# Modulation sums of the four late groups: 16 split fp32r products in one strip of rows become 8 plain fp32 products in four column groups

## The chip, the cores and the metric

The kernel runs on one core of one Trainium2 chip. The metric is device microseconds (us) of one execution. Before the change the median of 3 runs is 2868.03 us (2867.95 to 2868.06).

## The reference, cut to what matters

The program is one layer of a hybrid trunk: adaLN modulation, an input projection, a recurrent branch and a differential attention branch, an output projection, and an expert-choice mixture of 16 experts. The change touches only how the modulation vectors are made:

```
def modulation(cvec, w_mod, b_mod):
    m = jax.nn.silu(cvec) @ w_mod + b_mod
    return m[..., None, :]
...
sh1, sc1, g1, sh2, sc2, g2 = jnp.split(mod, 6, axis=-1)
h = rmsnorm(x, lp['g_pre1']) * (1 + sc1) + sh1
t, k, v, h_fin = token_mixer(h, ...)
x = x + g1 * rmsnorm(t, lp['g_post1'])
h = rmsnorm(x, lp['g_pre2']) * (1 + sc2) + sh2
f = expert_choice_ffn(h, ...)
x = x + g2 * rmsnorm(f, lp['g_post2'])
```

There are two conditioning vectors (latent and context, v = 0 and 1), D = 2048, and w_mod is 2048 x 12288. The first two of the six parts (sh1, sc1) are needed at once. The other four, "late groups" g = 0 to 3 (g1, sh2, sc2, g2), are needed only after the token mixer.

## The kernel before, in words

All work is in one program for five engines: TensorE (PE) multiplies, VectorE (DVE) and ScalarE (ACT) do elementwise work, and two queues start the transfers, SyncE (SP) for the large weights and GpSimd (POOL) for results and small loads. Every engine runs its own list in order and waits on semaphores.

A stage of 32 units makes the first 4096 columns of the input projection. A unit u is 128 columns of w_in. PE's loop in `block.tensor` runs over four groups g of eight units n, and for each unit over two halves of 320 tokens with 48 matmuls each (`unit_piece`, lines 2362 to 2364). Since fp32 weights are split in a high and a low fp32r part, ACT makes `w_hi` (`split_hi`, line 405) and DVE makes `w_lo` (`split_lo`, line 415) of a unit while PE works on the unit before; each is one instruction over 128x2048. `w_hi` and `w_lo` have two buffers, so the split of unit u + 1 starts when PE has left unit u - 1.

Beside this, group g also makes late modulation group g. The 16 row tiles of w_mod (128x2048, 1 MB each) go through three buffers `mod_raw`; SP issues their loads in `mod_tiles` (line 605). DVE multiplies each tile by the two columns of silu(c) and accumulates in `mod_acc` (`mod_tile`, lines 1559 and 1561, two instructions a tile). `MOD_TILES` says how many of the 16 tiles are taken in each of the eight units of a group: 3, 3, 3, 3, 2, 2, 0, 0. What is left is a sum over the 128 partitions, for two rows of 2048. For it ACT copies `mod_acc` to `acc_hi` at n = 6 (line 1071), DVE subtracts to `acc_lo` at n = 7 (`mod_low`, line 1576), and after unit 7 PE runs `sum_mod`: for four blocks of 512 columns and two v, a product with `acc_hi` and one with `acc_lo`, stationary `sel` 128x2, output on partitions 0 and 1 of PSUM banks 0 to 3 (lines 2375 and 2376). In unit 1 of the next group DVE adds the bias (`mod_row2`, line 1584), and POOL, which waits for it, stores the rows to `d_mod` (line 823).

`acc_hi` and `acc_lo` lie where `mod_raw` lies, so SP waits for the semaphore `mod_summed` before it loads the first three tiles of the next group (line 604).

After the 32nd unit PE runs the fourth sum and goes on with head 0 of the attention stage. After its third piece of 12 matmuls that head turns the keys (`keys`), which need `k_past` and `k`, loaded by POOL in its step u = 31 (lines 793 and 790).

Of the kernel before, what the change touches and what calls it, by code (L numbers as in the profile page):

```python
# [61 lines left out]
NMOD = 3  # L62
MOD_TILES = (3, 3, 3, 3, 2, 2, 0, 0)
MOD_FROM = [sum(MOD_TILES[:n]) for n in range(8)]

# [47 lines left out]
def trunk(nc, a, out_ctx, out_lat, out_k, out_v, out_state):  # L113
    ctx = ExitStack()
    with ctx:
# [42 lines left out]
        def place(at0, items):  # L158

            o, made = at0, {}  # L160
            for name, shape, dt in items:
# [14 lines left out]
                       ("sp_a", [P, 16], F32), ("sp_b", [P, 16], F32), ("sp_c", [P, 16], F32),  # L176
                       ("sp_d", [P, 16], F32), ("A1", [P, 2, KT], F32), ("ones2", [P, 4], F32)])
        mod_at = PLACED["ones2"] + 64
        A["sc"] = at("sc", [P, 32], F32, mod_at + NMOD * UB)
        sel = at("sel", [P, 2, 2], F32R, mod_at + NMOD * UB + 128)  # L180
        mod_raw = at("mod_raw", [P, NMOD, D], F32, mod_at)
# [3 lines left out]
        mod_acc = at("mod_acc", [P, 2, D], F32, s0 + 15360)  # L185
        acc_hi = at("acc_hi", [P, 2, D], F32R, mod_at)
        acc_lo = [at("acc_lo0", [P, D], F32R, mod_at + 2 * UB), at("acc_lo1", [P, D], F32R, s0)]
        m_row2 = at("m_row2", [2, D], F32, s0)
        m_row3 = at("m_row3", [2, D], F32, raw_at + 2 * UB)
        assert s0 + 15360 + 2 * UB <= PLACED["rows1"] and mod_at + NMOD * UB + 192 <= s_end  # L190
# [135 lines left out]
            "sqrt_x", "xn_ready", "x_turned", "xt_act", "xt_dve", "b_loaded", "m_row_ready", "m_stored",  # L326
            "zero_stored", "row_act", "start_used", "cols_taken", "mod_used", "mod_hi", "mod_lo", "mod_summed", "rows3_turned", "a1_ready", "tok_hi", "tok_lo",

# [227 lines left out]
        def _(sp):  # L556
# [39 lines left out]
            def mod_tiles(g, n):  # L596

                for k in range(MOD_FROM[n], MOD_FROM[n] + MOD_TILES[n]):
                    if k >= NMOD:
                        wait(sp, "mod_used", g * KT + k + 1 - NMOD)  # L600
                    else:
                        wait(sp, "mod_used", g * KT)
                        if g:
                            sp.wait_ge(S["mod_summed"], g)
                    sp.dma_start(mod_raw[:, k % NMOD, :], w_mod[k * P:(k + 1) * P, (g + 2) * D:(g + 3) * D]
                                 ).then_inc(mod_loaded[k % NMOD], 16)
# [129 lines left out]
        def _(pool):  # L736
# [59 lines left out]
            def load_values(h):  # L796
# [3 lines left out]
                               ).then_inc(S["v_loaded"], 16)  # L800

            for u in range(32):
                wait(pool, "in_taken", 2 * (u + 1))
                pool.dma_start(d_proj[u * P:(u + 1) * P, :], stage[:, u % 2, :]).then_inc(S["in_stored"], 16)
                if u == 31:
                    pool.wait_ge(S["mod_lo"], 8)
                    load_past(0)
                    load_rows(0, "k", 24, "k_loaded")
                stored("in_stored", (u + 1) * 16, "stage_free")
                if u == 26:  # L810
                    pool.wait_ge(S["zero_stored"], TT * 16)
                    load_recurrent(0)
                if u == 30:
                    pool.wait_ge(lo_ready, 2 * NRAW + 2 * (Q_IN * NRAW + 30 + 1))
                    pool.dma_start(m_row3[:], a["b_mod"][0:1, 5 * D:6 * D].to_broadcast([2, D])
                                   ).then_inc(S["b_loaded"], 16)
                if u % 8 == 7 and u < 31:
                    g = u // 8
                    pool.wait_ge(S["mod_summed"], g + 1)
                    pool.dma_start(m_row2[:], a["b_mod"][0:1, (g + 2) * D:(g + 3) * D].to_broadcast([2, D])  # L820
                                   ).then_inc(S["b_loaded"], 16)
                    wait(pool, "m_row_ready", g + 3)
                    pool.dma_start(d_mod[:, (g + 2) * D:(g + 3) * D], m_row2[:]).then_inc(S["m_stored"], 16)
            pool.sem_inc(phase, 1)
# [3 lines left out]
            wait(pool, "m_row_ready", 6)  # L828
            pool.dma_start(d_mod[:, 5 * D:6 * D], m_row3[:]).then_inc(S["m_stored"], 16)
            pool.wait_ge(S["m_stored"], 4 * 16)  # L830

# [140 lines left out]
        def _(act):  # L972
# [87 lines left out]
            for u in range(32):  # L1060
# [352 lines left out]
        def _(dve):  # L1413
# [7 lines left out]
            dve.memset(A["ones_row"][:], 1.0).then_inc(S["const_set"], 1)  # L1421
            own.done(dve.memset(A["ones2"][:], 0.0))
            own.settle()
            own.done(dve.memset(A["ones2"][:, 0:4:3], 1.0))
            own.settle()
            dve.tensor_copy(sel[:], A["ones2"][:].rearrange("p (v m) -> p v m", v=2)).then_inc(S["const_set"], 1)
            dve.wait_ge(S["rows_turned"], 1)
# [121 lines left out]
            def mod_tile(g, k):  # L1549
# [17 lines left out]

            def mod_low(g):

                dve.wait_ge(S["mod_hi"], g + 1)  # L1570
                if g == 0:
                    dve.wait_ge(S["v_stored"], 4 * 16)
                else:
                    dve.wait_ge(S["m_stored"], g * 16)
                for v in range(2):
                    TTn(acc_lo[v][:], mod_acc[:, v, :], acc_hi[:, v, :].bitcast(F32), ALU.subtract
                        ).then_inc(S["mod_lo"], 1)

            def mod_row2(g):

                dve.wait_ge(S["mod_summed"], g + 1)
                dve.wait_ge(S["b_loaded"], (g + 1) * 16)
                m = (m_row3 if g == 3 else m_row2)[:].rearrange("p (b n) -> p b n", b=4)
                TTn(m, ps[0:2, 0:4, :], m, ALU.add).then_inc(S["m_row_ready"], 1)

# [35 lines left out]
            for u in range(32):  # L1621
# [10 lines left out]
                if n == 7:  # L1632
                    mod_low(g)
                if u == 31:
# [20 lines left out]
            def head(h, final):  # L1655
# [89 lines left out]
                def take_T(qt):  # L1745

                    wait(dve, "pdT_hi", h * TT + qt + 1)
                    if qt == 0:
                        dve.wait_ge(S["m_stored"], 4 * 16)
                    if qt < TT - 1:  # L1750
# [464 lines left out]
        def _(pe):  # L2215
# [565 lines left out]
```

## Time and profile before

| what | value |
|---|---|
| median of 3 runs | 2868.03 us |
| span of the profiled execution | 2865.5 us |
| what lies around the span, as median less span | 2.5 us |
| PE busy | 2801.7 us, 98% of the span |
| DVE, ACT, POOL busy | 74%, 53%, 10% |
| stage of 32 units and four sums on PE | 194.0 to 663.5 us |
| granted TensorE clock, mean of the span | 0.991 of full speed |

The profile is of one execution, and its page gives the span from the first to the last instruction; the device time of that execution is taken as the span and the same 2.5 us around it. A matmul's row is its start and its modelled duration. Matmuls overlap, so what one costs is the distance from its start to that of the next, not its duration. Idle time in brackets stands before the row, with what ended it.

### The profile page before, as it was taken

How to read it: one execution, taken by the hardware profiler on the slowest of the kernel's cores; microseconds unless marked ns; L12 is line 12 of the kernel's file. 1: busy time of each engine (PE TensorE's matmuls, PEld its weight loads, DVE VectorE, ACT ScalarE, POOL GpSimd, SP SyncE). 2: the span in 40 equal slices, each digit the busy share in tenths (PEclk: the TensorE clock that was granted, in tenths of full speed). 3: DMA queues.
4: the chain of work that ended last, by engine and by line, in shares of the span. 5: the costliest groups of instructions: out<-in, count | busy, mean ns of one | idle time of the engine just before them, and what ended most of it. 6: DMA issues, size and time to landing. Idle time of an engine off the chain costs nothing.

```text
span 2865.5 us, 42985 instructions
## 1 busy us (share of the span) xinstructions
PE 2801.7 (98%) x15938; PEld 2465.4 (86%) x15938; DVE 2130.4 (74%) x1927; ACT 1512.7 (53%) x1484; POOL 285.5 (10%) x346
## 2 busy tenths in 40 slices
PE   7999999999999999999999996999999999999998
PEld 5689999999999999999998774888888888888886
DVE  2349779796777777763344577888888888888898
ACT  4411221215556655552233445777777777777776
POOL 1000000002111111100000001010111001110100
PEclk9999999999999999999999997999999999999999
DMA  9878669674343333364343766999999999999997
GB/s 367 312 268 258 225 190 303 206 236 143 123 122 115 116 118 114 110 208 135 119 137 121 267 233 247 362 396 395 396 396 397 390 395 395 394 390 386 391 393 298
DMA packets 301484, 757.07 MB, mean 264 GB/s; under 512 B 20376, under 2 KB 184768, under 8 KB 237072
## 3 DMA queue, kind: packets, MB, share of 16 engines
q1 hardware_dynamic: 277280, 650.01, 62.0%
q0 software_dynamic: 23200, 100.72, 10.9%
q10 hardware_dynamic: 928, 5.33, 0.5%
q8 instruction: 48, 0.79, 0.1%
q14 instruction: 28, 0.23, 0.0%
HBM read 700.61 MB, written 55.37 MB: 264 GB/s over the span
## 4 chain that ended last, share of the span: by engine, by line
PE 84%; DVE 8%; DMA 4%; issue 3%; ACT 1%; DVEq 0%; SPq 0%; ACTq 0%; POOLq 0%
PE ps L536 16%; PE ps L538 16%; PE ps L537 16%; PE ps L2362 8%; PE ps L2363 7%; PE ps L2364 7%; DVE mod_acc L1561 4%; PE ps L2493 3%; PE ps L2494 3%; PE ps L2495 3%; DMA mod_raw<-in_w_mod 2%; PE ps L2219 2%; DMA raw<-in_w_mod 1%; PE ps L2431 1%; DVE rsd L1787 1%
## 5 line engine op out<-in xcount | busy, mean ns | idle before, releaser
L461 DVE TENSOR_TENSOR we_lo<-raw,we_hi 128x2048 fp32r<-128x2048 f32 x384 | 877.2, 2289 | 114.3 <-ACT we_hi L456 113.9
L456 ACT ACTIVATE we_hi<-raw 128x2048 fp32r<-128x2048 f32 x384 | 736.5, 1919 | 261.0 <-PE ps L538 261.0
L2362 PE MATMUL ps<-hi,w_lo 128*128 128x320 f32 x2048 | 642.2, 314 | 3.4 <-DVE w_lo L415 3.4
L2363 PE MATMUL ps<-lo,w_hi 128*128 128x320 f32 x2048 | 632.7, 309 | 0.0
L2364 PE MATMUL ps<-hi,w_hi 128*128 128x320 f32 x2048 | 632.6, 309 | 0.0
L415 DVE TENSOR_TENSOR w_lo<-raw,w_hi 128x2048 fp32r<-128x2048 f32 x115 | 263.4, 2291 | 185.7 <-ACT w_hi L405 180.2
L536 PE MATMUL ps<-we_hi,xs_lo 128*128 128x512 f32 x1024 | 399.4, 390 | 0.1
L538 PE MATMUL ps<-we_hi,xs_hi 128*128 128x512 f32 x1024 | 399.2, 390 | 0.0
L537 PE MATMUL ps<-we_lo,xs_hi 128*128 128x512 f32 x1024 | 399.1, 390 | 0.0
L2362 PEld LDWEIGHTS ps<-hi,w_lo 128*128 128x128 f32 x2048 | 384.5, 188 | 12.6 <-issue 6.7
L2363 PEld LDWEIGHTS ps<-lo,w_hi 128*128 128x128 f32 x2048 | 384.7, 188 | 0.2
L2364 PEld LDWEIGHTS ps<-hi,w_hi 128*128 128x128 f32 x2048 | 384.5, 188 | 0.0
L405 ACT ACTIVATE w_hi<-raw 128x2048 fp32r<-128x2048 f32 x115 | 219.8, 1911 | 221.7 <-PE ps L538 135.3
L1561 DVE SCALAR_TENSOR_TENSOR mod_acc<-mod_raw,sc,mod_acc 128x2048 f32<-128x2048 f32 x120 | 276.7, 2347 | 4.9 <-DMA mod_raw<-in_w_mod 1.0
L536 PEld LDWEIGHTS ps<-we_hi,xs_lo 128*128 128x128 f32 x1024 | 192.7, 188 | 41.8 <-issue 0.7
L538 PEld LDWEIGHTS ps<-we_hi,xs_hi 128*128 128x128 f32 x1024 | 192.7, 188 | 40.2
L537 PEld LDWEIGHTS ps<-we_lo,xs_hi 128*128 128x128 f32 x1024 | 192.7, 188 | 39.5
L536 PE MATMUL ps<-we_hi,hid_lo 128*128 128x512 f32 x512 | 201.3, 393 | 0.4 <-DVE hid_lo L2126 0.4
L538 PE MATMUL ps<-we_hi,hid_hi 128*128 128x512 f32 x512 | 199.5, 390 | 0.0
L537 PE MATMUL ps<-we_lo,hid_hi 128*128 128x512 f32 x512 | 199.3, 389 | 0.0
L2493 PE MATMUL ps<-hi,w_lo 128*128 128x320 f32 x512 | 158.5, 310 | 0.3 <-DVE mix L1829 0.2
L2495 PE MATMUL ps<-hi,w_hi 128*128 128x320 f32 x512 | 158.2, 309 | 0.0
(439 smaller groups left out, 3877.4 us busy)
## 6 DMA issues: line engine op xcount, KB each, us to landing
raw<-in_w_e_gate SPq DMA_DIRECT2D x128, 1024.0 KB, 8.0
raw<-in_w_e_up SPq DMA_DIRECT2D x128, 1024.0 KB, 7.6
raw<-in_w_e_down SPq DMA_DIRECT2D x128, 1024.0 KB, 12.0
raw<-in_w_in SPq DMA_DIRECT2D x144, 512.0 KB, 5.4
mod_raw<-in_w_mod SPq DMA_DIRECT2D x64, 1024.0 KB, 5.4
raw<-in_w_mod SPq DMA_DIRECT2D x64, 512.0 KB, 7.5
raw<-in_w_o SPq DMA_DIRECT2D x64, 512.0 KB, 4.9
d_proj<-stage POOLq DMA_DIRECT2D x32, 320.0 KB, 3.4
```

Source lines behind the costliest of these rows:

```text
L415: dve.tensor_tensor(w_lo[:, j % NHL, s], raw[:, slot, s], w_hi[:, j % NHL, s].bitcast(F32), ALU.subtract).then_inc(lo_ready, 1 if fine else 2)
L456: act.activation(we_hi[:, k % NEH, :], raw_slot(k), ACT.Copy).then_inc(hi_ready, 2)
L461: TTn(we_lo[:, k % NEH, :], raw_slot(k), we_hi[:, k % NEH, :].bitcast(F32), ALU.subtract).then_inc(lo_ready, 2)
L536: pe.matmul(out, s_lo, m_hi, start=start, stop=False)
L537: pe.matmul(out, s_hi, m_lo, start=False, stop=False)
L538: return pe.matmul(out, s_hi, m_hi, start=False, stop=stop)
L1561: last = STT(mod_acc[:, v, :], w, c, mod_acc[:, v, :], ALU.mult, ALU.add)
L2362: pe.matmul(out, wl, hi[:, k, ms], start=(k % 16 == 0), stop=False)
L2363: pe.matmul(out, wh, lo[:, k, ms], start=False, stop=False)
L2364: last = pe.matmul(out, wh, hi[:, k, ms], start=False, stop=(k == KT - 1))
L2493: pe.matmul(out, wl, hi[:, k, ms], start=(kk == 0), stop=False)
L2495: last = pe.matmul(out, wh, hi[:, k, ms], start=False, stop=(kk == 7))
```

## The change

The low part, the high part and `sel` go. PE waits for `mod_used`, the count of tiles accumulated, and multiplies `mod_acc` itself, as plain fp32. The stationary operand is 32 columns wide (`pick_row`: a window of a row of zeros with a one at column 1, so that v lands on row v of each strip), the output block j of 512 columns goes to partitions 32j to 32j + 31 of PSUM bank 0. The bias and the rows of the result have the same layout, so the bias is loaded and the result stored by two transfers each, onto a tile that POOL clears first. `mod_raw` is no longer shared; only DVE's first product of a group waits for `mod_summed`. The tiles are spread as 2, 2, 3, 2, 2, 3, 2, 0. POOL's first loads for head 0 wait for the fourth sum, and no longer for the low part of it.

```
-MOD_TILES = (3, 3, 3, 3, 2, 2, 0, 0)
+MOD_TILES = (2, 2, 3, 2, 2, 3, 2, 0)
...
-        acc_hi = at("acc_hi", [P, 2, D], F32R, mod_at)
-        acc_lo = [at("acc_lo0", [P, D], F32R, mod_at + 2 * UB), at("acc_lo1", [P, D], F32R, s0)]
-        m_row2 = at("m_row2", [2, D], F32, s0)
-        m_row3 = at("m_row3", [2, D], F32, raw_at + 2 * UB)
+        m_row2 = at("m_row2", [P, 512], F32, s0)
+        m_row3 = at("m_row3", [P, 512], F32, raw_at + 2 * UB)
...  (SP, mod_tiles)
                         wait(sp, "mod_used", g * KT)
-                        if g:
-                            sp.wait_ge(S["mod_summed"], g)
...  (SP, u == 31)
                     sp.wait_ge(S["mod_summed"], 4)
+                    sp.wait_ge(S["m_stored"], 3 * 32)
...  (POOL)
+            def load_bias(g, row):
+                pool.memset(row[:], 0.0).then_inc(pool_own, 1)
+                pool.wait_ge(pool_own, g + 2)
+                for v in range(2):
+                    pool.dma_start(row[v:P:32, :], quarters(a["b_mod"][0, (g + 2) * D:(g + 3) * D])
+                                   ).then_inc(S["b_loaded"], 16)
+            def store_modulation(g, row):
+                for v in range(2):
+                    pool.dma_start(quarters(d_mod[v, (g + 2) * D:(g + 3) * D]), row[v:P:32, :]
+                                   ).then_inc(S["m_stored"], 16)
...
                 if u == 31:
-                    pool.wait_ge(S["mod_lo"], 8)
+                    pool.wait_ge(S["mod_summed"], 4)
                     load_past(0)
...  (ACT)
-                if u % 8 == 6:
-                    wait(act, "mod_used", (u // 8 + 1) * KT)
-                    act.activation(acc_hi[:], mod_acc[:], ACT.Copy).then_inc(S["mod_hi"], 1)
...  (DVE, mod_tile)
                 if k:
                     own.settle()
+                elif g:
+                    dve.wait_ge(S["mod_summed"], g)
...
-            def mod_low(g):
-                dve.wait_ge(S["mod_hi"], g + 1)
-                ...
-                for v in range(2):
-                    TTn(acc_lo[v][:], mod_acc[:, v, :], acc_hi[:, v, :].bitcast(F32), ALU.subtract
-                        ).then_inc(S["mod_lo"], 1)
...  (DVE, mod_row2)
-                TTn(m, ps[0:2, 0:4, :], m, ALU.add).then_inc(S["m_row_ready"], 1)
+                TTn(m, ps[:, 0, :], m, ALU.add).then_inc(S["m_row_ready"], 1)
...  (PE, sum_mod)
-                pe.wait_ge(S["mod_lo"], (g + 1) * 2)
+                wait(pe, "mod_used", (g + 1) * KT)
...
-                for b in range(4):
-                    s = slice(b * 512, (b + 1) * 512)
-                    for v in range(2):
-                        pe.matmul(ps[0:2, b, :], sel[:, v, :], acc_hi[:, v, s], start=(v == 0), stop=False)
-                        last = pe.matmul(ps[0:2, b, :], sel[:, v, :], acc_lo[v][:, s], start=False, stop=(v == 1))
+                for v in range(2):
+                    for j in range(4):
+                        last = pe.matmul(ps[32 * j:32 * j + 32, 0, :], A["pick_row"][:, 1 - v:33 - v],
+                                         mod_acc[:, v, j * 512:(j + 1) * 512], start=(v == 0), stop=(v == 1))
```

On DVE, the end of group 0 and the start of group 1 (before; the two `w_lo` in one row are units 7 and 8, the third is unit 9):

```order
L415 TENSOR_TENSOR w_lo<-raw,w_hi 128x2048 x2
L1576 TENSOR_TENSOR acc_lo_92<-mod_acc,acc_hi 128x2048
L1576 TENSOR_TENSOR acc_lo_93<-mod_acc,acc_hi 128x2048
L415 TENSOR_TENSOR w_lo<-raw,w_hi 128x2048
L1559 TENSOR_SCALAR mod_acc<-mod_raw,sc 128x2048 x2
L1561 SCALAR_TENSOR_TENSOR mod_acc<-mod_raw,sc,mod_acc 128x2048 x4
L415 TENSOR_TENSOR w_lo<-raw,w_hi 128x2048
L1584 TENSOR_TENSOR m_row_94<-ps,m_row_94 2x2048
L1561 SCALAR_TENSOR_TENSOR mod_acc<-mod_raw,sc,mod_acc 128x2048 x6
```

The same place on DVE after the change (the first row is the last two tiles of group 0, at n = 6):

```order
L1569 SCALAR_TENSOR_TENSOR mod_acc<-mod_raw,sc,mod_acc 128x2048 x4
L412 TENSOR_TENSOR w_lo<-raw,w_hi 128x2048 x2
L1567 TENSOR_SCALAR mod_acc<-mod_raw,sc 128x2048 x2
L1569 SCALAR_TENSOR_TENSOR mod_acc<-mod_raw,sc,mod_acc 128x2048 x2
L412 TENSOR_TENSOR w_lo<-raw,w_hi 128x2048
L1581 TENSOR_TENSOR m_row_90<-ps,m_row_90 128x512
L1569 SCALAR_TENSOR_TENSOR mod_acc<-mod_raw,sc,mod_acc 128x2048 x4
L412 TENSOR_TENSOR w_lo<-raw,w_hi 128x2048
L1569 SCALAR_TENSOR_TENSOR mod_acc<-mod_raw,sc,mod_acc 128x2048 x6
```

Between `w_lo` of one unit and of the next there are now 4, 4, 6, 4, 4, 6, 4 and 0 products instead of 6, 6, 6, 6, 4, 4, 0 and 0, and the two subtractions are gone.

On POOL, the last units of the stage and the first loads of head 0 (before; `m_row_95` is `m_row3`):

```order
L804 DMA d_proj<-stage 128x640 x4
L815 DMA m_row_95<-in_b_mod 2x2048
L804 DMA d_proj<-stage 128x640
L793 DMA k_past<-in_cache_k 128x128
L790 DMA k<-d_proj 128x640
L790 DMA q_in<-d_proj 128x640
```

The same place on POOL after the change:

```order
L816 DMA d_proj<-stage 128x640 x4
L803 MEMSET m_row_91 128x512
L806 DMA m_row_91<-in_b_mod 4x512 x2
L816 DMA d_proj<-stage 128x640
L789 DMA k_past<-in_cache_k 128x128
L786 DMA k<-d_proj 128x640
L786 DMA q_in<-d_proj 128x640
```

The order of the loads is the same; what the load of `k_past` waits for is another semaphore.

## Rows read from the trace of the kernel before

**Rows 1.** The page: busy time (share of the span) and instructions of PE.
```profile
PE 2801.7 (98%) x15938; PEld 2465.4 (86%) x15938; DVE 2130.4 (74%) x1927; ACT 1512.7 (53%) x1484; POOL 285.5 (10%) x346
```

**Rows 2.** PE's waits, 190 to 680 us: us in total, times, longest.
```profile
PE ps L2362 <- DVE w_lo L415: 3.4, 3, 1.4
```

**Rows 3.** Timeline of PE, first sum: start us, us, engine, line, operation.
```profile
306.51 0.31 PE L2364 MATMUL ps<-hi,w_hi 128*128 128x320 f32 x1
306.66 0.39 PE L2375 MATMUL ps<-acc_hi,sel 128*2 128x512 f32 x1
...
310.13 0.39 PE L2376 MATMUL ps<-acc_lo,sel 128*2 128x512 f32 x1
...
310.36 0.30 PE L2362 MATMUL ps<-hi,w_lo 128*128 128x320 f32 x1
```

**Rows 4.** Timeline of PE, start stage: two modulation units between value products.
```profile
97.95 0.40 PE L538 MATMUL ps<-w_hi,hi 128*128 128x512 f32 x1
98.28 1.92 PE L2242 MATMUL ps<-raw,c 128*32 128x512 f32 x16
100.13 0.50 PE L536 MATMUL ps<-w_hi,lo 128*128 128x512 f32 x1
100.47 0.39 PE L537 MATMUL ps<-w_lo,hi 128*128 128x512 f32 x1
```

**Rows 5.** Timeline of PE, tail: plain fp32 products over the full width.
```profile
2851.81 1.88 PE L2750 MATMUL ps<-t_out,ident 128*128 128x512 f32 x4
2853.53 1.88 PE L2753 MATMUL ps<-gained,spread 128*128 128x512 f32 x4
```

**Rows 6.** Timeline of DVE, group 1.
```profile
309.20 2.29 DVE L415 TENSOR_TENSOR w_lo<-raw,w_hi 128x2048 fp32r<-128x2048 f32 x1 [3.88 <-ACT w_hi L405]
315.72 2.48 DVE L1559 TENSOR_SCALAR mod_acc<-mod_raw,sc 128x2048 f32<-128x2048 f32 x2 [4.22 <-DMA mod_raw<-in_w_mod]
...
365.17 14.02 DVE L1561 SCALAR_TENSOR_TENSOR mod_acc<-mod_raw,sc,mod_acc 128x2048 f32<-128x2048 f32 x6
379.39 2.29 DVE L415 TENSOR_TENSOR w_lo<-raw,w_hi 128x2048 fp32r<-128x2048 f32 x1 [0.20 <-DVE mod_acc L1561]
381.60 9.31 DVE L1561 SCALAR_TENSOR_TENSOR mod_acc<-mod_raw,sc,mod_acc 128x2048 f32<-128x2048 f32 x4
```

**Rows 7.** Timeline of the SP queue, start of group 1.
```profile
310.61 1.29 SPq L605 DMA_DIRECT2D mod_raw<-in_w_mod  x3
```

**Rows 8.** Stretch of group 0's eight units: us, busy of PE, PEld, DVE, ACT, POOL.
```profile
194.00:306.50 112.50, 112.50 (x768) 112.47 (x767) 94.82 (x44) 24.63 (x24) 5.20 (x9) 1.00 0.70 222
```

**Rows 9.** Timeline of PE, start of unit 5 of group 1.
```profile
380.60 0.31 PE L2364 MATMUL ps<-hi,w_hi 128*128 128x320 f32 x1
381.82 0.41 PE L2362 MATMUL ps<-hi,w_lo 128*128 128x320 f32 x1 [0.92 <-DVE w_lo L415]
382.07 0.30 PE L2363 MATMUL ps<-lo,w_hi 128*128 128x320 f32 x1
```

**Rows 10.** Timeline of POOL and PE, end of the stage and head 0.
```profile
661.32 0.55 POOL L793 DMA_DIRECT2D k_past<-in_cache_k  x1
661.86 0.54 POOL L790 DMA_DIRECT2D k<-d_proj  x1
663.31 0.40 PE L2376 MATMUL ps<-acc_lo,sel 128*2 128x512 f32 x1
668.84 0.27 PE L2219 MATMUL ps<-ident,k_past 128*128 128x128 f32 x1
```

**Rows 11.** Tile k, 655 to 680 us; then issues by line, whole run.
```profile
DMA to landing us min/median/max: 3.3/3.3/3.3
...
k<-d_proj POOLq DMA_DIRECT2D x8, 320.0 KB, 5.0
```

**Rows 12.** Line 2242, all of its loads: duration ns min/median/max.
```profile
L2242 PEld LDWEIGHTS ps<-raw,c x256: 106/109/178, 10.5 to 118.1; 128*32 128x32 f32 x128
```

**Rows 13.** The page: GB/s moved in 40 slices.
```profile
GB/s 367 312 268 258 225 190 303 206 236 143 123 122 115 116 118 114 110 208 135 119 137 121 267 233 247 362 396 395 396 396 397 390 395 395 394 390 386 391 393 298
```

More of the change, by code:

```diff
@@ L176, in trunk @@
                        ("sp_a", [P, 16], F32), ("sp_b", [P, 16], F32), ("sp_c", [P, 16], F32),
-                       ("sp_d", [P, 16], F32), ("A1", [P, 2, KT], F32), ("ones2", [P, 4], F32)])
-        mod_at = PLACED["ones2"] + 64
+                       ("sp_d", [P, 16], F32), ("A1", [P, 2, KT], F32), ("pick_row", [P, 48], F32)])
+        mod_at = PLACED["pick_row"] + 192
         A["sc"] = at("sc", [P, 32], F32, mod_at + NMOD * UB)
-        sel = at("sel", [P, 2, 2], F32R, mod_at + NMOD * UB + 128)
         mod_raw = at("mod_raw", [P, NMOD, D], F32, mod_at)
@@ L326, in trunk @@
             "sqrt_x", "xn_ready", "x_turned", "xt_act", "xt_dve", "b_loaded", "m_row_ready", "m_stored",
-            "zero_stored", "row_act", "start_used", "cols_taken", "mod_used", "mod_hi", "mod_lo", "mod_summed", "rows3_turned", "a1_ready", "tok_hi", "tok_lo",
+            "zero_stored", "row_act", "start_used", "cols_taken", "mod_used", "mod_summed", "rows3_turned", "a1_ready", "tok_hi", "tok_lo",
             "bank_done", "bank_taken", "v_stored", "in_a_done", "in_taken", "in_stored",
@@ L800, in load_values, with quarters @@
                                ).then_inc(S["v_loaded"], 16)
+            def quarters(x):
+                return x.rearrange("(j n) -> j n", j=4)
+            def load_bias(g, row):
[8 more added lines that the diff above has]
+                                   ).then_inc(S["m_stored"], 16)
             for u in range(32):
@@ L814, in _ @@
                     pool.wait_ge(lo_ready, 2 * NRAW + 2 * (Q_IN * NRAW + 30 + 1))
-                    pool.dma_start(m_row3[:], a["b_mod"][0:1, 5 * D:6 * D].to_broadcast([2, D])
-                                   ).then_inc(S["b_loaded"], 16)
+                    load_bias(3, m_row3)
                 if u % 8 == 7 and u < 31:
                     g = u // 8
-                    pool.wait_ge(S["mod_summed"], g + 1)
-                    pool.dma_start(m_row2[:], a["b_mod"][0:1, (g + 2) * D:(g + 3) * D].to_broadcast([2, D])
-                                   ).then_inc(S["b_loaded"], 16)
+                    if g:
+                        pool.wait_ge(S["m_stored"], g * 32)
+                    load_bias(g, m_row2)
                     wait(pool, "m_row_ready", g + 3)
-                    pool.dma_start(d_mod[:, (g + 2) * D:(g + 3) * D], m_row2[:]).then_inc(S["m_stored"], 16)
+                    store_modulation(g, m_row2)
             pool.sem_inc(phase, 1)
@@ L828, in _ @@
             wait(pool, "m_row_ready", 6)
-            pool.dma_start(d_mod[:, 5 * D:6 * D], m_row3[:]).then_inc(S["m_stored"], 16)
-            pool.wait_ge(S["m_stored"], 4 * 16)
+            store_modulation(3, m_row3)
+            pool.wait_ge(S["m_stored"], 4 * 32)
             def load_head(h):
@@ L1421, in _ @@
             dve.memset(A["ones_row"][:], 1.0).then_inc(S["const_set"], 1)
-            own.done(dve.memset(A["ones2"][:], 0.0))
+            own.done(dve.memset(A["pick_row"][:], 0.0))
             own.settle()
-            own.done(dve.memset(A["ones2"][:, 0:4:3], 1.0))
-            own.settle()
-            dve.tensor_copy(sel[:], A["ones2"][:].rearrange("p (v m) -> p v m", v=2)).then_inc(S["const_set"], 1)
+            dve.memset(A["pick_row"][:, 1:2], 1.0).then_inc(S["const_set"], 1)
             dve.wait_ge(S["rows_turned"], 1)
@@ L1566, in mod_tile @@
                 wait(dve, "mod_used", g * KT + k + 1)
-            def mod_low(g):
-                dve.wait_ge(S["mod_hi"], g + 1)
[L1571 to L1574, printed above, removed]
-                for v in range(2):
-                    TTn(acc_lo[v][:], mod_acc[:, v, :], acc_hi[:, v, :].bitcast(F32), ALU.subtract
-                        ).then_inc(S["mod_lo"], 1)
             def mod_row2(g):
                 dve.wait_ge(S["mod_summed"], g + 1)
-                dve.wait_ge(S["b_loaded"], (g + 1) * 16)
-                m = (m_row3 if g == 3 else m_row2)[:].rearrange("p (b n) -> p b n", b=4)
-                TTn(m, ps[0:2, 0:4, :], m, ALU.add).then_inc(S["m_row_ready"], 1)
+                dve.wait_ge(S["b_loaded"], (g + 1) * 32)
+                m = (m_row3 if g == 3 else m_row2)[:]
+                TTn(m, ps[:, 0, :], m, ALU.add).then_inc(S["m_row_ready"], 1)
             prm, att = C["prm"], C["att"]
@@ L1631, in _ @@
                         conv(0, step)
-                if n == 7:
-                    mod_low(g)
                 if u == 31:
@@ L1748, in take_T @@
                     if qt == 0:
-                        dve.wait_ge(S["m_stored"], 4 * 16)
+                        dve.wait_ge(S["m_stored"], 4 * 32)
                     if qt < TT - 1:
```

## The prediction

> **What bounds the kernel now.** I read the busy times first: PE is busy for 2801.7 of 2865.5 us [rows 1], so a microsecond moves the end only if PE spends or waits it, and DVE, ACT and POOL count only where PE waits for them. Then I read PE's waits in the stage that the change touches. They are three waits for `w_lo`, 3.4 us in all [rows 2]. Last I read the timeline at one sum, at one of the waits, and at the entry to head 0. The reader should see there that PE goes from the last matmul of unit 7 into the sum with no gap and from the sum straight into the next unit [rows 3]: the sum lies on the path with all its length, and what prepares it (ACT's copy, DVE's two subtractions) doesn't.
>
> **The sum on PE.** Before: from the first product at 306.66 to the first matmul of the next unit at 310.36, 3.70 us for 16 products of 512 columns [rows 3]. There are four such sums, and the other three have the same form.
>
> After: 8 plain fp32 products, stationary 128x32, moving 128x512, onto four strips of 32 partitions of one bank, two rounds that accumulate. The trace has just that form in the start stage: line 2242. Two modulation units in a row are 8 such products, recorded as 16 since each fp32 product leaves two records. They stand between fp32r products: last one before at 97.95, the 16 records from 98.28, first one after at 100.13, the next at 100.47 [rows 4]. A product of 512 columns takes 0.231 us from start to start (3.70 / 16). So the eight take from 97.95 + 0.23 = 98.18 to 100.47 - 0.23 = 100.24, that is 2.06 us, with what it costs to enter and leave. That the four strips run side by side follows from the full-width fp32 product: 1.72 us for two of them, 0.86 each [rows 5], so eight in a row would be 6.9 us, and eight in four strips 1.7 us, which with 0.33 us of entry and exit is the 2.06.
>
> The gain is 3.70 - 2.06 = 1.64 us a sum, 6.6 us for four. Its bounds: 3.70 - 1.72 = 1.98 us a sum if entry and exit cost nothing (7.9), and 1.2 us a sum if the change between forms costs twice what the row shows (4.8). I take 6.6.
>
> [...]
>
> **The three waits.** Before, DVE falls behind in units 0 to 4 of groups 1 to 3. Its first tile waits 4.22 us for a transfer [rows 6] that SP could issue only at 310.61, behind `mod_summed` [rows 7]. Then each unit of three tiles takes DVE 14.02 + 0.20 + 2.21 = 16.43 us (365.17 to 381.60) [rows 6]. Eight PE units are 768 matmuls in 112.5 us, 14.06 a unit [rows 8]. DVE has `w_lo` of unit 5 ready at 381.6, and PE begins that unit 1.22 us after its last matmul instead of 0.15, and its second comes 0.25 instead of 0.15 us later [rows 9]: 1.07 + 0.10 = 1.17 us. The page counts 0.92 there, since a modelled end runs past the next start; so the three that it puts at 3.4 us are worth about 3.4 + 3 x 0.25 = 4.2 us.
>
> After, I follow DVE from the start T of PE's unit 0 in group 1. PE leaves unit 7 at T - 2.1. ACT's and DVE's splits of unit 9 follow that by 4.7 us before (306.7 to 311.4) [rows 3, 6], so DVE is free at T + 2.6. The tiles are there, since their buffers are free from the end of group 0. Two tiles with the first product (2.48 for two of line 1559, 4.67 for two of line 1561): T + 10. Each later `w_lo` is ready at its unit's start + 4.6 at best. A unit of two tiles costs DVE 2.2 + 9.5 = 11.7 us, of three 16.4. At n = 2 DVE starts `w_lo` at T + 30.5 and is done with three tiles at T + 47; it makes `w_lo` for unit 4 at T + 49.2, due at T + 56.2. At n = 5 the same: done at T + 89, `w_lo` for unit 7 at T + 91.5, due at T + 98.4. The least margin is 7 us, so all three waits go, 4.2 us. With the last tile at T + 101 and the sum at T + 112.4, the new wait for `mod_used` is over 11 us early. Bounds: 0 (waits stay) and 4.2.
>
> **What lies beside other work.** ACT loses a copy of 128x4096 and DVE two subtractions of 128x2048 a group; DVE's bias add goes from 2048 to 512 elements a partition. PE waited for none of them [rows 2], so they count 0; the smaller add only widens DVE's margin. POOL gets a memset and two small transfers more a group; it works behind PE and its loads in the stage have two buffers of `stage` for cover. If that cover were gone, the cost would be the 1 to 1.5 us that they issue for, each group, on ACT's copies, not on PE at first.
>
> **The moved wait at head 0.** Before, POOL issues `k_past` at 661.32 and `k` at 661.86, behind the store of unit 31, and the keys are turned at 668.84 [rows 10]. After, both stand behind the fourth sum. With the end E of unit 31 at 659.84 (663.31 + 0.23 - 3.70), the sum ends at E + 2.1, POOL sees it some 0.4 us later, issues `k_past` at E + 2.5 and `k` at E + 3.0, where before it was E + 2.0. `k` lands 3.3 us after issue as it did here, or 5.0 as in the median of eight [rows 11]: E + 6.3 to E + 8.0. The keys are due at E + 2.1 + 5.3 = E + 7.4. So the price is 0 to 0.6 us; behind it only the third piece of head 0 and what follows on PE would queue. I take 0, the near value being that of this very load. `q_in`, `gr` and `v` wait for the store of unit 31 as before, and SP's `rope` for `mod_summed`, as before.
>
> **Sum.** 6.6 + 4.2 - 0 = 10.8 us. Against the profiled execution, span 2865.5 and 2.5 around it, 2868.0 - 10.8 = 2857.2 us; the median of the runs, 2868.03, is the same to 0.1, so I predict 2857.2.
>
> **Rivals.**
> *The waits stay.* If the three-tile units or SP's order still make DVE late once a group, only the sums pay: 2868.0 - 6.6 = 2861.4. For it: a three-tile unit is still longer than a PE unit, by 2.4 us. Against it: each is followed by units 2.4 us shorter than PE's, and the late start by 4.22 us is gone. 0.10.
> *Head 0 starves.* The loads land late by 0.6 to 1.5 us; 2858 to 2859. For it: margin of only 1.1 us at the fast landing. 0.09.
> *The strips take turns.* If the four strips shared the array one after another for these operands (they have the same stationary window and all stream one tile, unlike line 2242), a sum would take 8 x 0.86 + 0.3 = 7.2 us in place of 3.70, 14 us more in four, less 4.2 of waits: 2877.8, slower. It decides once a sum is over 3.70 + 4.2 / 4 = 4.75 us. Against it stands the row of the same form. 0.04.
> *The loads of the strips don't hide.* If each of the 16 loads of 0.107 us [rows 12] stood alone, a sum would be 1.72 + 0.3 + 1.7 = 3.7 us, no gain on it, and the total 4.2: 2863.8. The rows speak against it: 16 records with their loads fit in 1.85 us, 0.13 over the bare streaming. [...] 0.03.
> *Given back later.* The experts' stage moves 390 to 397 GB/s [rows 13] and might set the end by itself. Against it: those loads follow PE's use of the buffers, so they come earlier with it. If it held for half the gain: 2862.6 to 2868. 0.05.
>
> **How the numbers follow.** The forecast as worked out has 0.69, with its own range 2855.5 to 2859.0 (bounds 7.9 and 4.8 for the sums, entry 0 to 0.6). I widen to 2854.5 at the low side, for a microsecond of what I can't see, and to 2862.5 at the high side, which takes in the waits that stay and head 0. Below the 0.2% line, 5.7 us, which is about what a measurement of this kernel tells from no change, lies everything under 2862.3: 0.69 + 0.10 + 0.09 and a little of the last, 0.89. Same 0.06, from the loads and the giving back. Slower 0.05.
>
> **What would show it.** In the profile after: eight products (16 records) of form 128*32, 128x512 per sum, about 2.1 us from the last matmul of unit 7 to the first of the next unit; no PE wait for `w_lo` in the stage; DVE's first tile of a group waiting for no transfer; stage end at 663.5 - 10.8 = 652.7 us; ACT without the copy of 128x4096; PE's turn of `k_past` 5.3 us after head 0 begins. The prediction is wrong if a sum takes over 2.6 us, if a wait for `w_lo` or for `mod_raw` on DVE still reaches PE, if head 0 opens with a wait, or if the stage ends 10 us earlier and the end of the program doesn't.

## The result

| kernel | median (us) | lowest to highest | executions |
|---|---|---|---|
| before | 2868.42 | 2866.02 to 2875.65 | 20 |
| after | 2873.99 | 2871.65 to 2875.72 | 20 |

After over before is 1.0017, with a 95% interval of 1.001 to 1.0023: slower by about 5 us, where 2857.2 was predicted. The time lies outside the range. The direction, slower, had a chance of 0.05; by the line of 0.2% (5.7 us) that the prediction draws, this is "same", which had 0.06.

### The profile page after: what moved, and what is told of

It is laid out like the page before. It is cut to its first block, busy times and chain, and to the rows that moved or that the text cites. A ratio compares the mean times of both kernels' runs of the same rounds, so it can differ in the third digit from the quotient of the medians.

```text
span 2873.9 us, 42975 instructions
## 1 busy us (share of the span) xinstructions
PE 2801.5 (97%) x15938; PEld 2466.8 (86%) x15938; DVE 2107.7 (73%) x1918; ACT 1498.9 (52%) x1480; POOL 293.3 (10%) x358
## 3 DMA queue, kind: packets, MB, share of 16 engines
q0 software_dynamic: 23456, 100.72, 10.8%
## 4 chain that ended last, share of the span: by engine, by line
PE 91%; DVE 4%; DMA 2%; ACT 2%; issue 2%; SPq 0%; DVEq 0%; ACTq 0%; POOL 0%; POOLq 0%
PE ps L533 16%; PE ps L535 16%; PE ps L534 16%; PE ps L2357 10%; PE ps L2359 10%; PE ps L2358 10%; PE ps L2487 3%; PE ps L2489 3%; PE ps L2488 3%; PE ps L2214 2%; PE ps L2425 1%; DMA raw<-in_w_mod 1%; DVE rsd L1782 1%; PE ps L2237 1%; PE ps L2226 1%
```

## The profile after

The page, to be set beside [rows 1], and one DMA queue. The queue's columns are packets, MB and share of the 16 engines; its packets of 16 KB are the fetches of instructions, of which the kernel before made 48.

```profile
span 2873.9 us, 42975 instructions
PE 2801.5 (97%) x15938; PEld 2466.8 (86%) x15938; DVE 2107.7 (73%) x1918; ACT 1498.9 (52%) x1480; POOL 293.3 (10%) x358
q8 instruction: 75, 1.23, 0.2%
```

PE's waits from 190 to 690 us, where [rows 2] had three of 3.4 us in all:

```profile
PE ps L2357 <- DVE w_lo L412: 10.9, 3, 3.7
PE ps L2214 <- DMA k<-d_proj: 1.3, 1, 1.3
```

The view still shows three waits for `w_lo`, three times as long. The timelines of PE and DVE at the first sum, to be set beside [rows 3] and [rows 6], show that they aren't the old ones: they stand behind the sums, not in the middle of a group.

```profile
307.98 0.31 PE L2359 MATMUL ps<-hi,w_hi 128*128 128x320 f32 x1
308.22 1.92 PE L2369 MATMUL ps<-mod_acc,pick_row 128*32 128x512 f32 x16
313.82 0.63 PE L2357 MATMUL ps<-hi,w_lo 128*128 128x320 f32 x1 [3.68 <-DVE w_lo L412]
314.25 0.47 PE L2358 MATMUL ps<-lo,w_hi 128*128 128x320 f32 x1
314.51 0.47 PE L2359 MATMUL ps<-hi,w_hi 128*128 128x320 f32 x1
...
319.40 0.31 PE L2357 MATMUL ps<-hi,w_lo 128*128 128x320 f32 x1
```

```profile
310.66 2.29 DVE L412 TENSOR_TENSOR w_lo<-raw,w_hi 128x2048 fp32r<-128x2048 f32 x1 [11.75 <-ACT w_hi L402]
312.87 2.82 DVE L1567 TENSOR_SCALAR mod_acc<-mod_raw,sc 128x2048 f32<-128x2048 f32 x2
```

The releaser that the profile names is a wrong one. The `w_lo` of 310.66 is that of unit 9; the one that PE's matmul at 313.82 reads, of unit 8, DVE began at 296.6 and had by 298.9. PE had its data for 15 us and stood still 3.68 us. What it waited for is in the rows of PE's sequencer (PEldq), which hold PE's semaphore waits, register operations and branches. Line 2374 is the `Fori` of the loop over the groups, and its `COMPARE_BRANCH` is the branch at the end of a turn. Here are the whole run and then the first turn alone (duration ns min/median/max, starts in us):

```profile
L2374 PEldq COMPARE_BRANCH  x4: 83/4996/5030, 308.3 to 669.0; - x4
```

```profile
L2374 PEldq COMPARE_BRANCH  x1: 5030/5030/5030, 308.3 to 308.3; - x1
```

The same line of the kernel before:

```profile
L2380 PEldq COMPARE_BRANCH  x4: 83/210/240, 306.5 to 659.7; - x4
```

The branch back to the loop's start took 5.0 us in each of three turns, where it took 0.21 to 0.24; the fourth, not taken, costs 0.08 in both. The first one ended at 313.36, and the next matmul began 0.46 us later. Between 305 and 330 us the instruction queue moved four blocks of 16 KB after the change, and between 300 and 330 none before:

```profile
q8 instruction: 4, 0.07, 1.6%
```

Windows around the first stall (us, busy of PE, PEld, DVE, ACT, POOL, granted clock, DMA share, GB/s), and the second window of the second turn:

```profile
308.00:313.80 5.80, 2.14 (x18) 0.44 (x17) 3.14 (x2) 2.23 (x2) 0.61 (x2) 0.87 0.40 146
313.80:319.20 5.40, 5.38 (x20) 5.38 (x21) 5.31 (x4) 0.00 (x0) 2.25 (x3) 0.50 0.49 147
319.20:325.00 5.80, 5.80 (x42) 5.80 (x41) 1.20 (x1) 0.44 (x1) 0.00 (x0) 1.00 1.11 353
```

```profile
434.60:440.00 5.40, 5.40 (x26) 5.40 (x27) 5.31 (x4) 0.00 (x0) 2.28 (x3) 0.68 0.47 144
```

After the 3.7 us in which PE was idle the granted clock is 0.50 of full speed: matmuls of 320 columns follow each other by 0.267 us instead of 0.147 for 20 of them, 2.4 us more. That is why PE's busy time hardly fell although its work did.

The fourth sum leaves the loop and doesn't branch back. Behind it stands what was forecast for all four; then comes the turn of the keys, with a wait (beside [rows 10]); and the load of `k` took 5.7 us (beside [rows 11]):

```profile
668.85 1.92 PE L2369 MATMUL ps<-mod_acc,pick_row 128*32 128x512 f32 x16
670.70 0.41 PE L2357 MATMUL ps<-hi,w_lo 128*128 128x320 f32 x1
...
677.50 0.33 PE L2214 MATMUL ps<-ident,k_past 128*128 128x128 f32 x1 [1.26 <-DMA k<-d_proj]
```

```profile
671.10 0.56 POOL L789 DMA_DIRECT2D k_past<-in_cache_k  x1 [0.84 <-PE ps L2369]
671.65 0.54 POOL L786 DMA_DIRECT2D k<-d_proj  x1
```

```profile
DMA to landing us min/median/max: 5.7/5.7/5.7
```

The account of the two profiled executions, by the start of the sums: before 306.66, 424.16, 542.15, 659.84, distances of 117.50, 117.99, 117.69; after 308.22, 429.05, 548.96, 668.85, distances of 120.83, 119.91, 119.89. The three turns lost 3.33 + 1.92 + 2.20 = 7.45 us. The stage began 1.46 us later, which lies ahead of all that is changed; the fourth sum gained 1.6 and head 0 lost 1.4. Together that is 8.7 us, where the spans differ by 8.4.

## The experiments

Three theories stood at first. A, placement: the branch costs a fetch because of where the loop lies among the blocks in which PE's instructions are fetched. B, the sum itself: its products in column groups hold the sequencer, and what comes behind them is late wherever it lies. C, the reading that the profile itself gives: DVE is late with `w_lo`. A became D in the course of this. A fetch is one packet of 16 KB, a block. In the placed kernel that comes next the last six of the first turn begin from 198.62 to 290.57 us, 18.4 us apart in the mean, and a turn has 1598 records of PE and takes 114.69 us; so a block holds 256 instructions (18.39 x 1598 / 114.69), an estimate that takes one record for one instruction. D supposes that PE keeps eight such blocks, and that the loop, of 1598 instructions, ends just inside its eighth; some time after the sequencer enters that block the ninth is fetched over the first. By D a branch back that comes sooner finds the first block (below, a hit), and a later one has to fetch it (a miss).

**after_slot176.** The loop's first instruction is put at place 176 of a block, so that the loop lies in seven blocks (176 + 1598 = 1774 of 1792). Nothing else changes.

```
-            with pe.Fori(0, 4) as g:
+            with nc.Fori(0, 4, engines=[mybir.EngineType.PE], head_slot={mybir.EngineType.PE: 176}) as g:
```

> The changed kernel, with PE's loop of the 32 units loaded so that its first instruction stands at slot 176 of a block of 256 instructions (1598 instructions, so it ends at slot 1774 of 1792 in its seventh block). Nothing else differs. Theory A (place of the loop in the fetched blocks): the backward branch, 5.03 us three times in the changed kernel against 0.24 before, hits again, the instruction queue q8 moves 48 packets and not 75, no half clock in the stage; time 2874.0 less 3 x 3.7 us of waiting and some 6 us of half clock, that is 2857 to 2860. Theory B (the column-group products in front of the branch hold PE's sequencer, wherever the loop lies): the branch stays at 5 us, 2873 to 2875. Theory C (DVE is late with w_lo, as the page's releaser says): nothing changes, 2874.

Measured: 2858.41 us (2857.29 to 2859.47), ratio to before 0.9964 (0.9949 to 0.9978; the brackets behind a ratio are its 95% interval). The branches, the queue, and the timeline at the first sum:

```profile
L2374 PEldq COMPARE_BRANCH  x5: 83/215/339, 190.1 to 650.9; - x5
```

```profile
q8 instruction: 49, 0.80, 0.1%
```

```profile
306.52 0.31 PE L2359 MATMUL ps<-hi,w_hi 128*128 128x320 f32 x1
306.76 1.92 PE L2369 MATMUL ps<-mod_acc,pick_row 128*32 128x512 f32 x16
308.62 0.42 PE L2357 MATMUL ps<-hi,w_lo 128*128 128x320 f32 x1
```

The fifth branch is the one into the placed loop. The sums stand 114.69, 114.68 and 114.69 us apart: 768 matmuls in 112.5 and 2.2 for the sum, with no wait in between. Against the unplaced kernel a turn lost 3.74 us of idle and 2.4 of half clock in the first, 3.7 and 1.5 in the other two, 16.5 us in all; the medians differ by 15.6. B, the sum as the cause wherever the loop lies, falls, and C with it.

**before_slot176.** The same placement in the kernel before: is it worth something by itself?

> The kernel before, with the start of PE's late loop placed so that neither the loop's last instructions nor its branch come near the end of the eighth block of 256 instructions. It is the control of the placement alone. Theory D (a missed loop back edge is what costs, and the kernel before hits all three of its own by default): three branches of 0.21 to 0.24 us as before, 48 or 49 instruction fetches, and the kernel before's time, 2868 us within 0.2%; the runs of the kernel before that lie up to 7 us above its median (2875.65 us was the slowest) should be missing here if they were executions in which back edges missed. Rival (the placement itself is worth the 10 us that the changed kernel gained by it): 2858 us.

Measured: 2867.39 (2866.34 to 2869.32), ratio 0.9994 (0.9985 to 1.0003). No change: the placement by itself is worth nothing that these runs show, and it pays where the branch missed.

**before_slot216 and before_slot239.** The kernel before with its branch 22 and 45 instructions into the eighth block.

```
+            with nc.Fori(0, 4, engines=[mybir.EngineType.PE], head_slot={mybir.EngineType.PE: 216}) as g:
```

> The kernel before, with PE's loop of the 32 units moved to slot 216, so that it ends in its eighth block. Theory A: the backward branch takes 5 us in three of four turns and q8 moves some 75 packets; the branch is reached 3.9 us before the sum is through (306.49 to 310.36), so PE waits about 1.9 us a turn and the clock does not fall: 2868.0 + 3 x 1.9 = 2873.7. Theory B or C: no difference, 2868.

> The kernel before, with PE's loop at slot 239: its branch is instruction 45 of the eighth block, so the sequencer enters that block before the waits of the sum, over 1.1 us ahead of the branch (at slot 216 it entered it 22 instructions, some 0.7 us, ahead, and missed once in three). Theory D (the ring holds eight blocks; some time after the eighth is entered the ninth is fetched over the first; a branch that comes sooner still hits): three branches of about 5 us, 75 packets, PE waits 1.9 us a turn: 2873 to 2875. Rival D' (an eighth block costs at most a chance miss, whatever the time in it): one miss or none, 2868 to 2870.

Measured for 216: 2867.78 (2866.42 to 2877.87), ratio 1.0002 (0.9992 to 1.0011), one miss of three. For 239: 2872.21 (2870.0 to 2875.42), ratio 1.0009 (1.0 to 1.0018), three misses of three. That is less than theory A and theory D expected of either (2873.7, and 2873 to 2875). The branches of the second turn of the one, and of all turns of the other:

```profile
L2380 PEldq COMPARE_BRANCH  x1: 4467/4467/4467, 425.1 to 425.1; - x1
```

```profile
L2380 PEldq COMPARE_BRANCH  x5: 83/3328/3732, 191.5 to 664.8; - x5
```

So the old sum misses too once the branch is far enough in the block, and misses in some turns and hits in others with the branch 22 instructions in. The cost of a miss is less here. The old sum has 3.87 us of products queued behind its branch (306.49 to 310.36, [rows 3]), which hide one of 3.3 to 3.7 us but for 0.2; the new one has 1.75 (308.33 to 310.08). What shows is the loop's next block: with the loop's start at place 239 the first holds 17 instructions (256 - 239), and PE stands still again when it is through with them.

```profile
311.62 0.39 PE L2376 MATMUL ps<-acc_lo,sel 128*2 128x512 f32 x1
312.07 0.41 PE L2362 MATMUL ps<-hi,w_lo 128*128 128x320 f32 x1
...
313.05 0.31 PE L2362 MATMUL ps<-hi,w_lo 128*128 128x320 f32 x1
314.56 0.42 PE L2363 MATMUL ps<-lo,w_hi 128*128 128x320 f32 x1 [1.20 <-issue]
```

The sums stand 118.79, 119.10 and 118.96 apart, 1.2 us more than before, and the medians differ by 3.8. The three gaps are 1.2, 1.9 and 1.4 us; part of them is given back, since the waits for `w_lo` fall from 3.4 to 1.2 us. The instruction queue shows the ninth block as D has it. From 304 to 307.9 us, ahead of the first turn's branch at 307.97, it moves one block of 16 KB:

```profile
q8 instruction: 1, 0.02, 1.5%
```

It begins at 304.8, 3.2 us ahead of the branch, and the next one at 309.0, 1.0 us behind the branch's start. In the kernel after the two stand at 309.2 and 309.4, both behind the start of the branch (308.33); the turns that hit have neither.

**after_slot195.** The changed kernel with nothing but the branch in the eighth block.

> The changed kernel with the loop at slot 195: only the branch itself lies in the eighth block, so that block is entered less than 0.2 us ahead of it. Theory D: the branch hits three times (0.2 us, 49 packets), though the loop covers eight blocks as in the changed kernel: 2857 to 2860. Rival D'' (any loop that touches an eighth block misses with the new sum in front): 75 packets, 2872 to 2875.

Measured: 2858.11 (2856.76 to 2861.93), ratio 0.9956 (0.9939 to 0.9973); branches of 0.21 to 0.24 us, 49 fetches. This loop may touch its eighth block, if it leaves it at once.

**after_mid.** The sum stands between the two halves of unit 7, with 96 loads and matmuls between it and the branch.

```
-                sum_mod(g)
+                        if n == 7 and half == 0:
+                            sum_mod(g)
```

> The changed kernel, with the sum of a group put between the two halves of its unit 7, 7 us of matmuls ahead of the branch; same number of instructions in the loop, at the same place. Theory A: the branch still misses three times (5 us, 75 packets), but is now reached with a full queue of matmuls in front (about 3 us), so PE waits some 2 to 2.5 us a turn: 2865 to 2869. Theory B: the branch hits (0.24 us, 48 packets), 2857 to 2860. Theory C: 2874, since DVE's w_lo is as late.

Measured: 2871.2 (2869.52 to 2872.15), ratio 1.0006 (0.9997 to 1.0016), above the 2865 to 2869 of theory A: the idle came to 3.0 us, not 2 to 2.5, with the half clock behind it. The branches still take 4.9 to 5.1 us:

```profile
308.68 0.31 PE L2359 MATMUL ps<-hi,w_hi 128*128 128x320 f32 x1
311.81 0.55 PE L2357 MATMUL ps<-hi,w_lo 128*128 128x320 f32 x1 [2.81 <-issue]
312.15 0.47 PE L2358 MATMUL ps<-lo,w_hi 128*128 128x320 f32 x1
```

From 308.68 to 311.81 are 3.13 us where 0.15 is the pace, with the half clock behind them. The gap follows the branch, not the sum: from the branch's start at 306.3 PE had 2.5 us of matmuls queued. Here the profile says "issue" and names no engine, which is right. By D the branch is late by the time that the sequencer spends in the eighth block, and the last instructions of a half, whose loads begin 0.147 us apart like the matmuls (303.70 to 306.19 us), would spend it as well as the sum does. That is D's reading of the three misses; no row shows the entry into the block.

**after_wide.** The same eight products over the whole array, stationary 128x128, so without column groups.

```
-                        last = pe.matmul(ps[32 * j:32 * j + 32, 0, :], A["pick_row"][:, 1 - v:33 - v],
-                                         mod_acc[:, v, j * 512:(j + 1) * 512], start=(v == 0), stop=(v == 1))
+                        c = 127 - 32 * j - v
+                        last = pe.matmul(ps[:, 0, :], pick_wide[:, c:c + P],
+                                         mod_acc[:, v, j * 512:(j + 1) * 512], start=(v == 0 and j == 0),
+                                         stop=(v == 1 and j == 3))
```

> The changed kernel, with the eight plain fp32 products over the full array (stationary 128x128 with the one at column 32j + v, all eight accumulating in one bank) and not in column groups; same count of instructions, same place. The sum takes 8 x 0.86 = 6.9 us on PE and the sequencer isn't held by a change of the array's tiling. Theory A: the branch misses as before, hidden by the longer sum: 2874.0 less 3 x 3.7 and the half clock (6), plus 4 x 4.9 = 2876. Theory B: the branch hits, about the same time, 2876, but 48 packets and a branch of 0.24 us. Theory C: PE still waits 3.7 us for w_lo behind the sum, 2890.

Measured: 2877.97 (2877.3 to 2881.58), ratio 1.0032 (1.0019 to 1.0045), with branches of 5.4 to 5.6 us:

```profile
307.78 7.03 PE L2377 MATMUL ps<-mod_acc,pick_wide 128*128 128x512 f32 x16
314.25 0.72 PE L2364 MATMUL ps<-hi,w_lo 128*128 128x320 f32 x1
314.80 0.31 PE L2365 MATMUL ps<-lo,w_hi 128*128 128x320 f32 x1
```

The sum is 6.5 us, 0.81 a product, against 1.86 for four strips: the strips do run side by side, by a factor of 3.5. And the longest branches of all cost nothing. The first began at 307.6, ahead of the sum, and ended at 313.1, while products were still queued up to 314.25. The distance of 0.55 us behind the sum isn't the branch's: it stands behind the fourth sum too, which has no branch back.

```profile
672.77 0.71 PE L2364 MATMUL ps<-hi,w_lo 128*128 128x320 f32 x1
673.32 0.31 PE L2365 MATMUL ps<-lo,w_hi 128*128 128x320 f32 x1
```

A miss costs what stands out behind the work queued ahead of it.

**slot176_tiles.** The placed kernel with the old `MOD_TILES`, 3, 3, 3, 3, 2, 2, 0, 0.

> The changed kernel at slot 176 with the old spread of the tiles, 3, 3, 3, 3, 2, 2, 0, 0. If the three waits for w_lo went because the buffers are no longer shared, DVE begins its first tile some 4 us earlier than before and the third long unit is still in time by about 2 us: no wait, 2858.4 as at slot 176. If it is the new spread that removed them, they come back with 1.2 us each: 2862.

Measured: 2857.95 (2856.96 to 2860.91), ratio 0.9957 (0.9944 to 0.9969); PE waits nowhere for `w_lo`. DVE in group 1 starts its first tile at once, for which it had waited 4.22 us [rows 6]:

```profile
309.19 2.29 DVE L412 TENSOR_TENSOR w_lo<-raw,w_hi 128x2048 fp32r<-128x2048 f32 x1 [11.78 <-ACT w_hi L402]
311.39 2.48 DVE L1567 TENSOR_SCALAR mod_acc<-mod_raw,sc 128x2048 f32<-128x2048 f32 x2
```

So the new spread of the tiles isn't needed for the three old waits to go. That they went because `mod_raw` no longer shares its place with the low and high parts fits DVE's row, 4.22 us earlier; the new spread with the place still shared wasn't run.

**slot176_keys.** The placed kernel, with the keys of a head turned two pieces later.

```
-                head(h, {2: "keys", 3: "lru0", 4: "lru1", 10: "s0", ...
+                head(h, {3: "lru0", 4: "lru1 keys", 10: "s0", ...
```

> The changed kernel at slot 176 with the keys of a head turned behind its second recurrent product (piece 4) and not behind piece 2. The wait of 1.9 us for k at the entry of head 0 goes, and nothing else moves: 2858.4 - 1.9 = 2856.5. If the later turn makes DVE late for the scores of every head, it is slower than 2858.4.

Measured: 2858.14 (2857.08 to 2858.64), ratio 0.9957 (0.9945 to 0.997). PE's waits from 660 us on of the placed kernel, and from 665 of this one:

```profile
PE ps L2214 <- DMA k<-d_proj: 1.7, 1, 1.7
```

```profile
PE ps L533 <- DVE o_n L1786: 2.0, 7, 0.4
```

The wait for `k` goes, and 2.0 us of seven small ones come, one a head, so that the time stays what it was. The 2856.5 of the expectation was missed; its other case, that DVE is late in every head, is the one that came, and it took back just what the keys had gained.

**after_hint.** The changed kernel, unplaced, with one more instruction at the start of each turn, `BRANCH_PREFETCH_HINT` in the trace.

```
-            with pe.Fori(0, 4) as g:
+            with nc.Fori(0, 4, engines=[mybir.EngineType.PE], hint_back_edge=True) as g:
```

> [...] The body grows by an instruction or two, which moves the branch no further out of the eighth block than it was, so it would miss three times without the hint. [...] Rival (something else that lies at this place holds PE, and the placement at slot 176 only moved it away): 2874 us. If the hint is not heeded: 2874 us too, with branches of 5 us; if it is heeded but works late: 2 to 4 us a branch, 2865 to 2870 us.

Measured: 2857.92 (2857.61 to 2858.74), ratio 0.9963 (0.9949 to 0.9977).

```profile
L2374 PEldq BRANCH_PREFETCH_HINT  x4: 31/34/45, 190.7 to 537.2; - x4
...
L2374 PEldq COMPARE_BRANCH  x4: 80/228/262, 307.5 to 651.6; - x4
```

```profile
q8 instruction: 48, 0.79, 0.1%
```

The loop lies where it lay (in the first turn its blocks are fetched 94.9, 76.0, 57.7, 35.2 and 19.9 us ahead of the branch, and 94.5, 76.2, 58.0, 35.8 and 19.8 in the kernel after), the branch comes as late as there, 2.6 us behind the sequencer's last wait, and it hits, in 0.22 to 0.26 us. So neither the place nor the sum loses time by itself; by D it is the missing first block alone. D gave this run the time of the placed kernel, 2858.4 us within 1.5, and that came, and 75 fetches or more, and those didn't: there are 48. From 288 us to the end of the loop no block is fetched, where the kernel after made 27 fetches more than these 48. How the hint brings this about no row shows. Both repairs beat both kernels by 10 us or more, and between them there is no difference that these runs show.

## Why the prediction was wrong

**The step that failed** is the sum's price as "from the first product to the first matmul of the next unit", 3.70 before and 2.06 after, with PE going "from the sum straight into the next unit". It took the distance for the products' own length; measured, it was 5.60 in the first turn. The loop's branch lies in it, and only the products queued behind it hide it. For a branch of 0.21 us that needs no word; the change made it one of 5.0 and cut what hides it from 3.87 to 1.75 us; 5.03 + 0.46 to begin again - 1.75 is the 3.74 of the first turn. With the other two turns that is 11.1 us, and 5.4 us of half clock. The text asked of each edit what hides it, and never of the loop: it read PE's waits and matmuls, and not its sequencer.

**Why the branch became late.** The sequencer's last wait ahead of the sum, before, after and in after_wide, and the branch of after_wide:

```profile
L383 PEldq EVENT_SEMAPHORE  x1: 51/51/51, 305.5 to 305.5; - x1
```

```profile
L380 PEldq EVENT_SEMAPHORE  x1: 51/51/51, 305.7 to 305.7; - x1
```

```profile
L381 PEldq EVENT_SEMAPHORE  x1: 51/51/51, 305.4 to 305.4; - x1
L2383 PEldq COMPARE_BRANCH  x1: 5454/5454/5454, 307.6 to 307.6; - x1
```

Before, the branch comes 1.0 us after that wait (306.5); after, 2.6 us (308.3). Between them lie the products of the sum. The loop's instructions lie in the same places in both: 1922 records of PE stand ahead of it and 1598 in a turn. after_wide has the new products without column groups, and its branch comes 2.2 us after the wait and misses three times. So 1.2 of the 1.6 us come with the plain fp32 products as such, and 0.4 with their standing in column groups. Why the sequencer is held at them stays open.

The prediction weighed entry to the strips and exit from them as time of the array, 0.33 us, and that was right: the sum before head 0 came to 2.09 us. It never asked what the products do to the sequencer. By D these 1.6 us are what moved three hits to three misses, which is argued and not shown by itself: after_slot176 has the same 2.6 us and hits, so the delay costs nothing without the place, and before_slot239 misses with 1.0 us, by more instructions in the block.

**What is shown of D, and what isn't.** Shown: with the branch before or at the start of the eighth block the new sum's loop hits; the old sum's misses one time of three with the branch 22 instructions in, and three of three with 45; with the hint the branch hits. The place of the unplaced loop should lie between the last two: of the blocks fetched in the first turn the earliest and the latest begin 91.6 and 20.9 us ahead of its branch, for 89.4 and 20.1 at place 216 and 94.8 and 21.6 at 239. A missed turn fetches nine blocks, the ninth and the loop's eight; that the ninth is written over the first is inferred from this. Fetches follow a taken branch: 27 of 16 KB more, 9 a turn, with branches of 5 us. And a loop of 1598 instructions goes round three times without a fetch when it lies in seven blocks (after_slot176, none from 290.6 to 652.8 us) and when its branch opens an eighth (after_slot195, none from 293.5 to 655.4 us), so that at least the eight blocks of that loop were held. That PE keeps eight and not more is D's supposition; the ninth fetch of a missed turn fits it.

**What held.** The sum: 2.09 us on leaving the loop, and 2.2 between units in the placed kernel, for 2.06. The strips side by side: 1.86 against 6.5 us. Their loads hide: 16 of 0.11 us lie within these 1.86. The three waits: gone, 4.2 us. ACT's and DVE's smaller work: worth nothing that the sum leaves room for. Nothing was given back in the experts' stage. The margins at `mod_used`: no wait. The stage ends at 652.7 us in the placed kernel, as forecast. (A slip of the working changes nothing: T + 91.5 should be T + 91.2.) By these the placed kernel should have 10.8 us less than before, and with the 1.9 us of head 0 below 8.9; the spans of the profiled executions differ by 8.8 and the medians by 10.0.

**What was mis-sized.** Head 0, taken as 0 with 0.6 at most. `k` was issued where forecast (E + 2.9, E being 668.76, the end of the last unit) but took 5.7 us to land here and 6.2 in the placed kernel, against 3.3 in [rows 11] and 5.0 in the median of eight. The wait was 1.3 to 2.2 us in all runs of the changed kernel that load `k` behind the sum and turn the keys where they stood. The moved wait did more than delay the issue. SP starts the loads of `k_turn` behind the same sum; before, 2.3 us after `k` had gone out at 661.86 [rows 10], after, 0.4 us ahead of it, so that `k` shares the engines with them. Before, and after:

```profile
664.12 2.30 SPq L618 DMA_DIRECT2D k_turn<-d_proj  x4
```

```profile
671.21 1.85 SPq L614 DMA_DIRECT2D k_turn<-d_proj  x4
```

That this made the landing late is argued from these rows. after_mid speaks for it: there the fourth sum comes 7 us sooner, the loads of `k_turn` go out at 661.45 and `k` at 668.70, `k` lands after 3.4 us, and PE doesn't wait for it. No run was made for this alone.

**The rivals.** None had the mechanism. "The strips take turns" gave the right sign for a wrong reason, and its own sign of truth, a sum over 4.75 us, was there (5.60 from 308.22 to 313.82), which shows why a total is no proof of its cause: the row of the fourth sum, 1.85, was needed to tell them apart. A rival that belonged there, by D: a branch back of a long loop whose first block is no longer held, with the price of a miss less the work queued behind it.

## What to carry to other kernels

Where an edit touches the last instructions of a long loop, read the sequencer's branch row before and after, and ask what array work is queued behind that branch; a faster operation hides less. A wait whose named releaser ended long before has another cause, here the fetch of instructions, and a wait that appears in every turn but the last points to the branch back. Place such a loop, or hint its branch, before judging what is in it: the same change was worth +5.6 us or -10.0 us by that alone.

## What the runs showed that was not expected

- A taken branch with fetches of the loop's blocks behind it (a miss) took 3.3 to 5.6 us on PE, against 0.21 to 0.24, and 0.22 to 0.26 with the hint.
- Whether it misses depends on more than the layout: with one layout (place 216) the kernel before missed once in three turns. The kernel before has single executions up to 2875.65 us, and placed at 176 none of 11 over 2869.32; that these are missed branches would fit, but 11 executions are few, and only the profiled ones have a trace.
- Idle stretches of PE of 3.0 to 3.7 us were each followed by a lower granted clock for 3.4 to 5.4 us of work (in the kernel after 0.50 from 313.8 to 319.2 us, and 0.68 from 434.6 to 440.0); after the 1.2 us in the first turn of before_slot239, and the 1.9 us in its second, the clock stayed full (1.00 from 311.5 to 320 us and from 430 to 440 us).
- Eight plain fp32 products, 128x512 moving, took 1.86 us in four column groups and 6.5 us over the whole array. Both hold the sequencer, 2.6 and 2.2 us from its last wait to the branch, where the 16 split products let it through in 1.0.
